# Layer 0 attention: pages issued by one engine, a ring of seven groups, the set-up moved

## The chip, the cores and the metric

The kernel runs on one core of a Trainium2 chip. A core has five engines with queues of their own: PE (matmul), DVE (VectorE), ACT (ScalarE), POOL (GpSimd) and SP, which only issues transfers and waits. They meet through semaphores. Sixteen DMA engines carry out what any of them issues. The metric is device time in microseconds of one execution, median of several.

## The reference, cut to what matters

One step of a two-layer decoder, for a prompt of 512 tokens and for 8 samples with 4 new tokens each. Layer 0 mixes two things: attention with forgetting (8 heads of 64) and a pooling mixer. The samples attend over 2048 past tokens, which lie in 16 pages of 128 tokens each, found through a page table.

```python
def gather_pages(pool, page_table):
    g = pool[page_table]
    return g.reshape((page_table.shape[0], page_table.shape[1] * pool.shape[1]) + pool.shape[2:])

def fox_attention(q, k, v, logf, pos0):
    cum = jnp.cumsum(logf.astype(jnp.float32), axis=1).transpose(0, 2, 1)
    ...
        logits = jnp.einsum('bqhd,bkhd->bhqk', qi, k, preferred_element_type=jnp.float32) * scale
        logits = logits + ci[..., :, None] - cum[:, :, None, :]
        mask = (k_pos[None, :] <= q_pos[:, None])[None, None]
        p = masked_softmax(logits, mask)
        return jnp.einsum('bhqk,bkhd->bqhd', p.astype(v.dtype), v)
```

For the samples k and v are the gathered pages of `cache_fox_k` and `cache_fox_v` with the new rows behind them: 8 samples x 16 pages x 2 caches = 256 pages, each 128 tokens x 512 numbers of 4 bytes, 256 KB.

## The kernel before

`fox_mixer` runs layer 0's mixer in stages, one behind the other, with all engines meeting between two stages (a stage's end clears its semaphores on POOL). The stages that matter here are the pooling mixer (`pooling`, 218 to 251 us of the trace) and the attention (`fox_prompt`, 252 to 512 us). Behind it comes the output projection.

In the attention stage two things share the engines. `prompt_attention` does the prompt: 8 heads x 4 tiles of 128 queries are 32 units, plus four "out" items, one item per step, and the phases of an item (scores, maximum, exponential, turn, values) lie some steps apart. Scores are four matmuls a unit: the query against the key's high part (KH) and low part (KL), a bias (SELB against B3, the sum of the forget gates in three parts) and a mask (ID against MASK). The keys' parts are made by ACT (L1739, L1740) and DVE (L1784, L1785), the queries by POOL (L1839, L1841).

Beside it `PastAttention` does the samples' past, in generators: each engine's generator moves one phase per step of the prompt, and runs on by itself when the prompt is done. A sample's 16 pages of keys are four groups of four pages, its values four more. The order of the 64 groups is fixed: keys of sample 0, then for each sample b the keys of b + 1 and the values of b. A turn is 11 phases: four with a key group, four with a value group, and three in which probabilities are turned and the output is finished. In the turn b = -1 only the keys of sample 0 are there, but it has 11 phases as well.

Groups land in a ring of four slots (`SLOTS`): two in RINGf and two in the free half of PT. `load` issues a group: for each page `value_load` reads the page's number into a register (L1336), then the page's transfer is issued (L1337). SP issues pages 0 and 2 of each group, POOL pages 1 and 3, each with a semaphore per slot. Group k waits until group k - 4 is used (`used`, raised by PE). SP issues the first four groups, then the stores of the new keys and values from TOK (`store_tokens`, which waits until they have landed), and then the rest. POOL first makes four queries and then issues, between its other work. PE waits for both halves in `landed`.

DVE starts the stage with its set-up (`setup` in `fox_prompt`): the values are copied to VE, B3 and SELB are made, then MASK and ID. Only then is `consts` raised, for which PE and ACT wait.

Of the kernel before, what the change touches and what calls it, by code (L numbers as in the profile page):

```python
# [999 lines left out]
class Mixers(Kernel):  # L1000
# [205 lines left out]
    def pooling(self, PT, meal):  # L1206
        nc, ps, i, o, H = self.nc, self.ps, self.i, self.o, self.H
        EX, NE = POOLW[-1] - 1, POOLW[-1] - 1 + TS
        with self.stage() as (sb, sem):
# [4 lines left out]
            ld, tr, ev, mm, st, dc, dd = (sem("pl_" + n) for n in ("ld", "tr", "ev", "mm", "st", "dc", "d"))  # L1214
            with nc.Block() as block:
# [14 lines left out]
                def _(pe):  # L1230
# [14 lines left out]
                    for g in range(4):  # L1245
# [4 lines left out]
                        last.then_inc(mm, 1)  # L1250

# [40 lines left out]

class PastAttention:

    R, PAGES, QUARTERS, SLOTS = FH * TS, PAST // PAGE, 4, 4
# [3 lines left out]
    def __init__(self, kernel, sb, sem, PT, TOK, NC, EP, first):  # L1299
# [4 lines left out]
        self.ring = sb("RINGf", [P, 2, self.QUARTERS, 512])  # L1304
# [9 lines left out]
        self.sp_full, self.pool_full = ([sem(f"fd_{n}_full{s}") for s in range(self.SLOTS)] for n in ("sp", "pool"))  # L1314
# [10 lines left out]
    def slot(self, k):  # L1325
        s = k % self.SLOTS
        return self.ring[:, s, :, :] if s < 2 else self.low[:, s - 2, :, :]

    def load(self, engine, parity, k):
        kind, b, n = self.groups[k]  # L1330
        if k >= self.SLOTS:
            engine.wait_ge(self.used, k - self.SLOTS + 1)
        pages = self.k.i["cache_fox_k"] if kind == "k" else self.k.i["cache_fox_v"][0].rearrange("n t h d -> n t (h d)")
        for a in range(parity, self.QUARTERS, 2):
# [3 lines left out]
                (self.pool_full if parity else self.sp_full)[k % self.SLOTS], 16)  # L1338

    def sp(self, sp, store):  # L1340
# [3 lines left out]
        for k in range(self.SLOTS):  # L1344
            self.load(sp, 0, k)
        store(sp)
        for k in range(self.SLOTS, len(self.groups)):
            self.load(sp, 0, k)
        self.k.start_out(sp, self.k.i["ab_w_out"][0], self.first)

    def pool(self, pool):
        for k in range(self.SLOTS):
            self.load(pool, 1, k)
        yield
        for b in range(-1, NB):
            for kind, of in (("k", b + 1), ("v", b)):
                for n in range(self.PER):
                    k = self.index.get((kind, of, n))
                    if k is not None and k + self.SLOTS < len(self.groups):
                        self.load(pool, 1, k + self.SLOTS)  # L1360
                    yield
            yield
            yield
            yield

    def pe(self, pe):
# [76 lines left out]
        for b in range(-1, NB):  # L1443
# [21 lines left out]
    def act(self, act):  # L1465
# [25 lines left out]
        for b in range(-1, NB):  # L1491
            for n in range(self.PER):
                yield
            for n in range(self.PER):
                if n == 0 and b + 1 < NB:
                    exponentials(b + 1)
                yield
# [9 lines left out]
    def dve(self, dve):  # L1507
# [50 lines left out]
        nc.vector.memset(RS[:, :], 0.0)  # L1558
        link(nc.vector.tensor_reduce(SAME[:, 0:R], self.k.ident.rearrange("p (a r) -> p r a", a=QUARTERS), AX.X, ALU.add))
# [10 lines left out]
        for b in range(-1, NB):  # L1570
# [4 lines left out]
            for n in range(self.PER):  # L1575
# [16 lines left out]
class Attention(Mixers):  # L1592

    def prompt_tiles(self, sb, sem, n_units, key_slots):
# [3 lines left out]
                 ID=sb("IDr", [P, P], F32R), MASK=sb("MASKr", [P, P], F32R), PC=sb("PC", [P, 3, P]))  # L1598
        T["KT"] = [(sb(f"KH{n}", [P, w], F32R), sb(f"KL{n}", [P, w], F32R)) for n, w in enumerate(key_slots)]
        names = ("consts", "queries", "q_high", "keys", "k_high", "scores", "maxima", "bank_read", "turned", "out_act", "out_dve", "valued", "combined",  # L1600
                 "added", "dc")
        return T, {n: sem("pa_" + n) for n in names}

    def prompt_attention(self, T, sems, groups, heads, keysets, outs, setup_dve, store, beside=None):
# [50 lines left out]
        with nc.Block() as block:  # L1655
# [5 lines left out]
            def _(pe):  # L1661
                if beside:
                    phases = beside.pe(pe)
                pe.wait_ge(sems["consts"], 1)
# [1258 lines left out]
```

## Time and profile before

| | |
|---|---|
| median of three runs | 2511.11 us (2507.73 to 2511.7) |
| span of the profiled execution | 2506.9 us |
| median less span | 4.2 us |
| PE busy | 2148.1 us (86%) |
| DVE, ACT, POOL busy | 1208.0, 579.4, 264.4 us |
| moved by DMA | 322.15 MB, mean 129 GB/s |
| attention stage of layer 0 | 251.97 to 511.88 us |
| pages moved in it | 256 x 256 KB |

The span runs from the first to the last instruction of the profiled execution; the runs' times have some start and end around it, so a change of the span is added to the median. Two views of the profile are used: groups (how much of a stretch an engine or the DMA engines were busy, who waited for whom, how long an instruction took) and the order of time. In the order of time "x4 3.70" stands for four instructions from the first one's start to the last one's end, and the brackets give the engine's idle time and what ended it. "SPq" is SP's queue of instructions.

### The profile page before, as it was taken

The numbers are of one execution on the slowest core, as the hardware profiler recorded it, in microseconds if no ns is written. First come the engines' busy times: TensorE is split into PE (matmuls) and PEld (weight loads), VectorE is DVE, ScalarE is ACT, GpSimd is POOL, SyncE is SP. The second block draws the span as 40 slices with busy tenths as digits, with TensorE's granted clock in tenths as the row PEclk, the third lists the DMA queues.
The fourth block names the chain that finished last, engine by engine and source line by source line (L and its number), as shares of the span: only waits on it lengthen the run. The fifth ranks groups of instructions, "written<-read, shape, count | busy, mean of one in ns | idle before, by whom it ended". The sixth has DMA issues, their size and how long they took to land. (4 is left out here: it accounts for less than half of the span.)

```text
span 2506.9 us, 49578 instructions
## 1 busy us (share of the span) xinstructions
PE 2148.1 (86%) x18597; PEld 1932.8 (77%) x18597; DVE 1208.0 (48%) x2280; ACT 579.4 (23%) x1074; POOL 264.4 (11%) x429
## 2 busy tenths in 40 slices
PE   4987697787999899698779996998987688999898
PEld 2863573475999899698469995988974487999898
DVE  4434531155444433443645657777743355444433
ACT  2220331012101000201135664444431211101000
POOL 0100423200000000000012222212223100000000
PEclk8986896688999999799779997998988898999999
DMA  9325778834323231223440003433448522223221
GB/s 354 112 63 220 242 246 322 308 118 136 92 84 92 84 101 52 62 68 113 203 151 2 1 2 112 123 115 103 121 160 324 216 64 74 86 85 91 87 92 59
DMA packets 237438, 322.15 MB, mean 129 GB/s; under 512 B 18235, under 2 KB 194440, under 8 KB 229807
## 3 DMA queue, kind: packets, MB, share of 16 engines
q1 hardware_dynamic: 215191, 239.29, 28.9%
q0 software_dynamic: 22048, 80.24, 9.3%
q8 instruction: 121, 1.98, 0.3%
q14 instruction: 78, 0.64, 0.1%
HBM read 311.56 MB, written 16.42 MB: 131 GB/s over the span
## 5 line engine op out<-in xcount | busy, mean ns | idle before, releaser
L441 PE MATMUL ps<-XHup,WHup 128*128 128x272 f32 x1408 | 293.2, 290 | 17.0 <-DVE XLup L415 13.5
L441 PE MATMUL ps<-XHup,WLup 128*128 128x272 f32 x1408 | 292.8, 290 | 0.0
L441 PE MATMUL ps<-XLup,WHup 128*128 128x272 f32 x1408 | 291.8, 289 | 0.0
L2279 PE MATMUL ps<-CHi,W1H 128*128 128x256 f32 x768 | 222.3, 289 | 37.5 <-DVE CLo L2382 37.5
L441 PEld LDWEIGHTS ps<-XHup,WHup 128*128 128x128 f32 x1408 | 222.7, 189 | 19.9 <-DVE XLup L415 14.3
L441 PEld LDWEIGHTS ps<-XLup,WHup 128*128 128x128 f32 x1408 | 222.7, 190 | 0.0
L441 PEld LDWEIGHTS ps<-XHup,WLup 128*128 128x128 f32 x1408 | 221.0, 190 | 0.0
L2280 PE MATMUL ps<-CLo,W1H 128*128 128x256 f32 x768 | 220.2, 287 | 0.0
L2281 PE MATMUL ps<-CHi,W1L 128*128 128x256 f32 x768 | 220.2, 287 | 0.0
L2279 PEld LDWEIGHTS ps<-CHi,W1H 128*128 128x128 f32 x768 | 150.5, 196 | 39.5 <-DVE CLo L2382 29.2
L434 DVE CAST WHup<-RAWup 128x1024 fp32r<-128x1024 f32 x88 | 61.1, 695 | 221.1 <-DMA RAWup<-in_w_up 164.5
L441 PE MATMUL ps<-GH,WHdn 128*128 128x272 f32 x704 | 148.5, 293 | 17.0 <-remote 15.1
L2280 PEld LDWEIGHTS ps<-CLo,W1H 128*128 128x128 f32 x768 | 150.4, 196 | 0.0
L2281 PEld LDWEIGHTS ps<-CHi,W1L 128*128 128x128 f32 x768 | 150.2, 196 | 0.0
L441 PE MATMUL ps<-GL,WHdn 128*128 128x272 f32 x704 | 147.4, 291 | 0.0
L441 PE MATMUL ps<-GH,WLdn 128*128 128x272 f32 x704 | 146.9, 290 | 0.0
L1797 DVE TENSOR_REDUCE NM<-ps 128x1 f32<-128x128 f32 (+1 forms) x224 | 89.6, 403 | 111.3 <-PE ps L1685 74.9
L441 PE MATMUL ps<-XHin,WHin 128*128 128x272 f32 x576 | 122.8, 295 | 19.3 <-issue 12.2
L1759 ACT ACTIVATE P<-ps,NM 128x128 f32<-128x128 f32 (+1 forms) x224 | 101.3, 458 | 139.3 <-DVE NM L1797 134.3
L441 PEld LDWEIGHTS ps<-GH,WHdn 128*128 128x128 f32 x704 | 112.5, 192 | 17.9 <-issue 17.9
L441 PE MATMUL ps<-XHin,WLin 128*128 128x272 f32 x576 | 121.3, 293 | 0.0
L441 PE MATMUL ps<-XLin,WHin 128*128 128x272 f32 x576 | 121.3, 293 | 0.0
(503 smaller groups left out, 4240.0 us busy)
## 6 DMA issues: line engine op xcount, KB each, us to landing
RAWup<-in_w_up SPq DMA_DIRECT2D x88, 512.0 KB, 3.8
Wearly<-in_w_mod SPq DMA_DIRECT2D x24, 1024.0 KB, 11.4
RAWdn<-in_w_down SPq DMA_DIRECT2D x14, 1408.0 KB, 6.5
RAWin<-in_nsa_w_in SPq DMA_DIRECT2D x20, 512.0 KB, 3.6
Wmod<-in_w_mod SPq DMA_DIRECT2D x8, 1024.0 KB, 16.9
RINGf<-in_cache_fox_k SPq DMA_DIRECT2D x32, 256.0 KB, 6.2
PT<-in_cache_fox_k SPq DMA_DIRECT2D x32, 256.0 KB, 6.1
RINGf<-in_cache_fox_k POOLq DMA_DIRECT2D x32, 256.0 KB, 5.7
```

Of the source, the lines that this page charges most:

```text
L434: link(self.nc.vector.tensor_copy(hi, values))
L441: mm = self.nc.tensor.matmul(self.ps[:, banks + n, 0:HALF], w, x[:, n * HALF:(n + 1) * HALF], start=start, stop=stop)
L1759: nc.scalar.activation(P3[:, n % 4, 0:w], ps[:, made[step] % S_BANKS, 0:w], ACT.Exp, bias=NM[:, n:n + 1]).then_inc(sems["bank_read"], 1)
L1797: nc.vector.tensor_reduce(NM[:, n:n + 1], ps[:, made[step] % S_BANKS, 0:width(*units[n])], AX.X, ALU.max, negate=True).then_inc(sems["maxi ...
L2279: nc.tensor.matmul(out, WH[:, sig, k, w], hi, start=(k == 0 and m == 0), stop=False, skip_group_check=True)
L2280: nc.tensor.matmul(out, WH[:, sig, k, w], lo, start=False, stop=False, skip_group_check=True)
L2281: last = nc.tensor.matmul(out, WL[:, sig, k, w], hi, start=False, stop=(k == KU - 1), skip_group_check=True)
```

## The change

- All 256 pages are issued by SP. `load` loses its `parity` and runs over all four pages; one semaphore per slot counts them. POOL's generator is gone.
- The ring has seven slots: three in RINGf, two in PT, and two more in TOK, whose rows are free once the stores have landed and the values are copied. `FIRST` is 5: SP issues five groups, then the stores, and groups 5 and 6 wait for `stored` and for the copy of the values.
- B3, SELB, ID and MASK are made by POOL in the pooling stage (`prompt_biases`); the tiles live in the outer stage.
- The values go to VE by ACT (`values`, behind the second key's copies); `consts` is not used where the samples' part runs beside the prompt. DVE clears QBA ahead of step 0.
- The turn b = -1 has 8 phases in place of 11: one in place of the four empty value phases.

```diff
-    def pooling(self, PT, meal):
+    def pooling(self, PT, meal, NC, bias):
...
+                @block.gpsimd
+                def _(pool):
+                    self.prompt_biases(pool, Chain(pool, made), PT, NC, *bias)
...
+    def prompt_biases(self, pool, link, PT, NC, B3, SELB, ID, MASK):
+        rest, middle, three = PT[0:FH, 8, 0:TP], PT[0:FH, 9, 0:TP].bitcast(F32R), PT[:, 10, 0:FH]
+        nc.gpsimd.tensor_copy(ID, self.ident)
+        nc.gpsimd.tensor_copy(MASK, self.dmask)
+        link(nc.gpsimd.tensor_tensor(three, self.ident[:, 0:FH], self.ident[:, 32:32 + FH], ALU.add))
+        link(nc.gpsimd.tensor_tensor(three, three, self.ident[:, 64:64 + FH], ALU.add))
+        nc.gpsimd.tensor_copy(SELB, three.unsqueeze(2).to_broadcast([P, FH, P]))
+        link(nc.gpsimd.tensor_scalar(B3, self.cos[:, 0:TP], 0.0, None, ALU.mult))
+        link(nc.gpsimd.tensor_copy(B3[0:FH, :], NC[:, 0:TP]))
+        link(nc.gpsimd.tensor_tensor(rest, NC[:, 0:TP], B3[0:FH, :].bitcast(F32), ALU.subtract))
+        link(nc.gpsimd.tensor_copy(middle, rest))
+        link(nc.gpsimd.tensor_copy(B3[32:32 + FH, :], middle.bitcast(F32)))
+        link(nc.gpsimd.tensor_tensor(B3[64:64 + FH, :], rest, middle.bitcast(F32), ALU.subtract))
...
-    R, PAGES, QUARTERS, SLOTS = FH * TS, PAST // PAGE, 4, 4
+    R, PAGES, QUARTERS, SLOTS, FIRST = FH * TS, PAST // PAGE, 4, 7, 5
...
+        self.rows_free = ((stored, 64), (valued, 1))
+        self.rows = TOK[:, 0:PT_TILES, :].rearrange("p t c -> p (t c)").rearrange("p (s a f) -> p s a f", s=2, a=self.QUARTERS)
...
-        return self.ring[:, s, :, :] if s < 2 else self.low[:, s - 2, :, :]
+        return self.ring[:, s, :, :] if s < 3 else self.low[:, s - 3, :, :] if s < 5 else self.rows[:, s - 5, :, :]
...
-    def load(self, engine, parity, k):
+    def load(self, engine, k):
         kind, b, n = self.groups[k]
         if k >= self.SLOTS:
             engine.wait_ge(self.used, k - self.SLOTS + 1)
+        elif k >= self.FIRST:
+            for signal, value in self.rows_free:
+                engine.wait_ge(signal, value)
...
-        for a in range(parity, self.QUARTERS, 2):
+        for a in range(self.QUARTERS):
             at = b * self.PAGES + self.PER * a + n
             page = engine.value_load(self.k.pages[0:1, at:at + 1], min_val=0, max_val=self.k.n_pages - 1)
             engine.dma_start(self.slot(k)[:, a, :], pages[ds(page, 1), :, :].rearrange("a p f -> p (a f)")).then_inc(
-                (self.pool_full if parity else self.sp_full)[k % self.SLOTS], 16)
+                self.full[k % self.SLOTS], 16)
...
-        for k in range(self.SLOTS):
-            self.load(sp, 0, k)
+        for k in range(self.FIRST):
+            self.load(sp, k)
         store(sp)
-        for k in range(self.SLOTS, len(self.groups)):
-            self.load(sp, 0, k)
+        for k in range(self.FIRST, len(self.groups)):
+            self.load(sp, k)
...
-    def pool(self, pool):
-        for k in range(self.SLOTS):
-            self.load(pool, 1, k)
...
         def landed(k):
-            pe.wait_ge(self.sp_full[k % self.SLOTS], 16 * QUARTERS // 2 * (k // self.SLOTS + 1))
-            pe.wait_ge(self.pool_full[k % self.SLOTS], 16 * QUARTERS // 2 * (k // self.SLOTS + 1))
+            pe.wait_ge(self.full[k % self.SLOTS], 16 * QUARTERS * (k // self.SLOTS + 1))
...
-            for n in range(PER):
+            for n in range(PER if b >= 0 else 1):
                 if b >= 0:
                     values(b, n)
...
+                        if values_act and k == keys_made[2]:
+                            values_act(act)
...
-            def setup(dve, link):
-                nc.vector.tensor_copy(VE[:, :, :, 0:HD], TOK[:, 0:PT_TILES, 512:1024].rearrange("p j (h d) -> p j h d", h=FH))
-                nc.vector.memset(VE[:, :, :, HD:HD + 1], 1.0)
...
+            def ones(dve, link):
+                nc.vector.memset(VE[:, :, :, HD:HD + 1], 1.0).then_inc(sems["values_dve"], 1)
+
+            def values(act):
+                nc.scalar.copy(VE[:, :, :, 0:HD], TOK[:, 0:PT_TILES, 512:1024].rearrange("p j (h d) -> p j h d", h=FH)).then_inc(sems["values_act"], 1)
```

On SP, at the first groups that wait for a used slot, the program before has two pages behind a wait (L1336 reads the number, L1337 issues):

```order
L1336 TENSOR_LOAD pages [waits fd_used_10]
L1336 ISA x2
L1337 ISA
L1337 DMA RINGf<-in_cache_fox_k 128x512
L1336 TENSOR_LOAD pages
L1336 ISA x2
L1337 ISA
L1337 DMA RINGf<-in_cache_fox_k 128x512
L1336 TENSOR_LOAD pages [waits fd_used_10]
```

and the changed program, where the two lines are L1361 and L1362, has four:

```order
L1361 TENSOR_LOAD pages [waits fd_used_10]
L1361 ISA x2
L1362 ISA
L1362 DMA RINGf<-in_cache_fox_k 128x512
L1361 TENSOR_LOAD pages
L1361 ISA x2
L1362 ISA
L1362 DMA RINGf<-in_cache_fox_k 128x512
...
L1361 TENSOR_LOAD pages [waits fd_used_10]
```

Two more pages stand there in the cut. The instructions of one page are the same five kinds in both.

On DVE, at the start of the attention stage, the program before has the set-up ahead of the first key's low part (L1784):

```order
L1869 COPY VE<-TOK 128x32x64
L1870 MEMSET VE 128x32
L1871 TENSOR_SCALAR B_10<-PT 128x512
...
L1879 CAST SELB<-three 128x1024
L85 ISA
L1775 CAST MASKr<-CN 128x128
L1776 CAST IDr<-CN 128x128
L85 ISA
L1784 TENSOR_TENSOR KL_10<-PT,KH_10 64x512
```

and the changed program has only clearing there:

```order
L1883 MEMSET VE 128x32
L1566 MEMSET QBA 128x1024
L1567 MEMSET RS 128x2
L1805 TENSOR_TENSOR KL_10<-PT,KH_10 64x512
```

The set-up's other instructions stand on POOL in the stage before, and the copy to VE on ACT behind its first exponential.

## Rows read from the trace of the kernel before

**Rows 1.** Busy us by stretch: PE PEld DVE ACT POOL (instructions), clock, DMA, GB/s
```profile
300.00:336.00 36.00, 31.66 (x337) 24.65 (x336) 13.17 (x35) 13.47 (x30) 12.28 (x20) 0.86 0.68 235
336.00:366.00 30.00, 28.53 (x342) 22.00 (x340) 12.98 (x38) 9.44 (x22) 8.58 (x16) 0.99 0.80 282
...
394.00:421.00 27.00, 20.30 (x234) 11.09 (x230) 3.47 (x14) 2.14 (x7) 8.58 (x16) 0.63 0.87 313
```

**Rows 2.** Waits of SP's queue, 250 to 515 us: total us, times, longest
```profile
SPq L1336 <- PE ps L1380: 69.8, 13, 15.6
SPq L1336 <- PE ps L1405: 18.1, 20, 1.8
```

**Rows 3.** Order of time, SP, start of stage: start, us, engine, line, operation
```profile
253.89 3.70 SPq L1337 DMA_DIRECT2D RINGf<-in_cache_fox_k  x4
...
258.35 3.63 SPq L1337 DMA_DIRECT2D PT<-in_cache_fox_k  x4
...
262.02 0.44 SPq L1195 DMA_DIRECT2D out_fox_k_p<-TOK  x1
...
274.79 3.71 SPq L1337 DMA_DIRECT2D RINGf<-in_cache_fox_k  x4
```

**Rows 4.** Lines L1336 and L1337, SP's queue: ns min/median/max
```profile
L1336 SPq TENSOR_LOAD <-pages x128: 262/269/498, 252.9 to 496.2; - x128
L1336 SPq FUSED_REGOPS  x128: 152/152/188, 253.4 to 496.5; - x128
...
L1337 SPq DMA_DIRECT2D RINGf<-in_cache_fox_k x32: 337/338/377, 253.9 to 462.0; - x32
```

**Rows 5.** Order of time, SP, later stretches
```profile
394.28 3.65 SPq L1337 DMA_DIRECT2D RINGf<-in_cache_fox_v  x4
...
398.70 3.64 SPq L1337 DMA_DIRECT2D PT<-in_cache_fox_v  x4
...
493.42 3.81 SPq L1337 DMA_DIRECT2D PT<-in_cache_fox_v  x4
...
1847.11 17.14 SPq L2155 DMA_DIRECT2D KS<-in_cache_nsa_ks  x16
```

**Rows 6.** Issue to landing, us: RINGf, 253 to 260; L1337, 394 to 403
```profile
DMA to landing us min/median/max: 2.7/2.9/3.1
...
DMA to landing us min/median/max: 2.6/5.3/6.4
```

**Rows 7.** Order of time, stage's start, and line L1999 of a later stage
```profile
252.02 1.67 DVE L1869 COPY VE<-TOK 128x2048 f32<-128x2048 f32 x1 [1.08 <-PEq L117]
...
252.69 2.11 POOL L1841 TENSOR_TENSOR QS<-PT,QS 64x512 fp32r<-64x512 f32 x1
...
263.23 0.25 DVE L1776 CAST IDr<-CN 128x128 fp32r<-128x128 f32 x1
...
266.36 0.44 PE L1680 MATMUL ps<-KH,QS 128*128 128x128 f32 x1 [16.25 <-DVE KL L1785]
...
L1999 ACT COPY VE<-TOK x2: 1037/1042/1047, 1244.2 to 1245.1; 128x1024 f32<-128x1024 f32 x2
```

**Rows 8.** Order of time, one turn's values and heads, and the stage's end
```profile
409.50 1.94 PE L1405 MATMUL ps<-PT,PTT 128*32 128x512 f32 x8 [0.61 <-DMA PT<-in_cache_fox_v]
...
411.37 1.91 PE L1415 MATMUL ps<-TOK,PTN 32*32 32x512 f32 x2
...
416.02 1.92 PE L1438 MATMUL ps<-SAME,Of 128*128 128x32 f32 x8
...
509.52 0.75 DVE L1546 TENSOR_SCALAR Of<-ps,W 128x512 f32<-128x512 f32 x1 [2.79 <-PE ps L1415]
...
511.53 0.35 DVE L1554 COPY H<-ps 64x16 f32<-64x16 f32 x2 [1.26 <-PE ps L1438]
```

**Rows 9.** Order of time, end of the pooling stage
```profile
237.74 0.17 DVE L1284 TENSOR_TENSOR Dl<-Dl,PT 128x16 f32<-128x16 f32 x1
...
244.87 5.24 PE L1249 MATMUL ps<-Dl,MAP 128*128 128x272 f32 x16
```

More of the change, by code:

```diff
@@ L1313, in __init__ @@
         self.const_in = sem("fd_const")
-        self.sp_full, self.pool_full = ([sem(f"fd_{n}_full{s}") for s in range(self.SLOTS)] for n in ("sp", "pool"))
+        self.full = [sem(f"fd_full{s}") for s in range(self.SLOTS)]
         self.used, self.queries, self.scores, self.maxima, self.probs = (sem("fd_" + n) for n in ("used", "queries", "scores", "maxima", "probs"))
@@ L1493, in act @@
                 yield
-            for n in range(self.PER):
+            for n in range(self.PER if b >= 0 else 1):
                 if n == 0 and b + 1 < NB:
@@ L1574, in dve @@
                 yield
-            for n in range(self.PER):
+            for n in range(self.PER if b >= 0 else 1):
                 if n == 1 and b >= 0:
@@ L1663, in _ @@
                     phases = beside.pe(pe)
-                pe.wait_ge(sems["consts"], 1)
+                else:
+                    pe.wait_ge(sems["consts"], 1)
                 for step in range(steps):
@@ L1684, in _ @@
                         if dense(g):
-                            last = nc.tensor.matmul(bank[:, i * P:w], ID[:, :], MASK[:, :], start=False, stop=True, skip_group_check=True)
+                            last = nc.tensor.matmul(bank[:, i * P:w], ID, MASK, start=False, stop=True, skip_group_check=True)
                         else:
-                            last = nc.tensor.matmul(bank[:, 0:span], ID[:, :], G["mask"][:, i, :], start=False, stop=True, skip_group_check=True)
+                            last = nc.tensor.matmul(bank[:, 0:span], ID, G["mask"][:, i, :], start=False, stop=True, skip_group_check=True)
                         last.then_inc(sems["scores"], 1)
@@ L1731, in _ @@
                     phases = beside.act(act)
-                act.wait_ge(sems["consts"], 1)
+                else:
+                    act.wait_ge(sems["consts"], 1)
                 for step in range(steps):
@@ L1774, in _ @@
                 setup_dve(dve, link)
-                nc.vector.tensor_copy(MASK[:, :], self.dmask)
-                link(nc.vector.tensor_copy(ID[:, :], self.ident))
-                dve.sem_inc(sems["consts"], 1)
+                if beside:
+                    next(phases)
+                else:
+                    nc.vector.tensor_copy(MASK, self.dmask)
+                    link(nc.vector.tensor_copy(ID, self.ident))
+                    dve.sem_inc(sems["consts"], 1)
                 for step in range(steps):
@@ L1826, in _ @@
                 placed = summed = 0
-                if beside:
-                    phases = beside.pool(pool)
                 for step in range(steps):
@@ L1853, in _, with fox_prompt @@
                         nc.gpsimd.tensor_tensor(dst, dst, T2[:, adds[g] % 2, :, :], ALU.add).then_inc(sems["added"], 1)
-                    if beside:
-                        next(phases, None)
-                for _ in phases if beside else ():
-                    pass
-    def fox_prompt(self, PT, TOK, NC, EP, first, store):
+    def fox_prompt(self, PT, TOK, NC, EP, bias, first, store, stored):
         nc, H = self.nc, self.H
         with self.stage() as (sb, sem):
-            T, sems = self.prompt_tiles(sb, sem, FH * PT_TILES, [TP] * 3)
-            past = PastAttention(self, sb, sem, PT, TOK, NC, EP, first)
+            B3, SELB, ID, MASK = bias
+            T, sems = self.prompt_tiles(sb, sem, FH * PT_TILES, [TP] * 3, (ID, MASK))
+            past = PastAttention(self, sb, sem, PT, TOK, NC, EP, first, stored, sems["values_act"])
@@ L1888, in fox_prompt @@
                                    value=lambda j, h=h: VE[:, j, h, :]))
-            self.prompt_attention(T, sems, groups, heads, keysets, [H[:, c, 0:TP] for c in range(4)], setup, lambda sp: past.sp(sp, store), past)
+            self.prompt_attention(T, sems, groups, heads, keysets, [H[:, c, 0:TP] for c in range(4)], ones, lambda sp: past.sp(sp, store), past, values)
     def gather(self, pool, table, col, where, dst, loaded):
@@ L1924, in fox_mixer @@
                 self.to_tokens(PT, 4, 8, TOK, 6)
-                self.pooling(PT, (self.early, 13))
-                self.fox_prompt(PT, TOK, NC, EP, first, lambda sp: self.store_tokens(sp, TOK, [("fox_k", 0, 512, 0), ("fox_v", 512, 512, 0)], stored))
+                self.pooling(PT, (self.early, 13), NC, bias)
+                self.fox_prompt(PT, TOK, NC, EP, bias, first,
+                                lambda sp: self.store_tokens(sp, TOK, [("fox_k", 0, 512, 0), ("fox_v", 512, 512, 0)], stored), stored)
 class Trunk(Attention):
```

44 lines of the change are left out of this document (15 added, 29 removed).

## The prediction

> **What bounds the kernel now.** I read three views in this order: the busy table of stretches, the waits of SP's queue, and the order of time. The change touches the layer 0 attention stage (252 to 512 us) and the end of the pooling stage before it. Nothing else moves, so the question is what sets the end of that stage. From 394 to 421 us, one sample's turn of eight page groups, PE is busy 20.3 of 27 us at a granted clock of 0.63, while the DMA engines are busy 0.87 of the time and move 313 GB/s [rows 1]: pages, not arithmetic. With prompt work beside it a turn takes 30 us (336 to 366, clock 0.99) and the first one 36 us [rows 1]. SP is not short of time now: it waits 69.8 + 18.1 us for a ring slot, that is for PE to finish with a group [rows 2]. POOL issues the other half of the pages. So today the rate comes from PE and the DMA engines together, through four slots, and SP has slack. The change takes away the half that gives SP its slack, so the first number that I need is the time that SP takes to issue one page.
>
> **SP's price of a page.** At the stage's start SP issues eight pages with no wait and no POOL beside it: the first starts at 253.89, the last ends at 258.35 + 3.63, so it starts at 261.64 (an issue is 0.338 us long [rows 4]); (261.64 - 253.89) / 7 = 1.107 us from one page to the next [rows 3]. Other stretches agree: four pages from 394.28 to 398.70 give 1.105, and sixteen pages of another cache (half the bytes) took 17.14, so (17.14 - 0.34) / 15 = 1.120 [rows 5]. The instructions themselves are shorter: 0.269 to read the page number, 0.152 for the address, 0.338 to issue [rows 4], 0.76 in sum with two tiny ones left out; the rest of the interval stands between them as time of the sequencer. The size of the transfer hardly enters. I take 1.107.
>
> **Part 1, all 256 pages on SP.** Before, SP and POOL issue 128 each. A group is four pages, 4.43 us of SP alone, and a turn of eight groups 35.4 us, against 27 to 30 us that a turn now takes. The issue becomes the bound. Its chain: first page at 253.89 as before (nothing of the change is ahead of it on SP). Five groups go ahead of the stores, 20 pages, the last at 253.89 + 19 x 1.107 = 274.92. The first store is issued 0.38 us behind the last page's start (before: 262.02 after 261.64), so at 275.30. From the first store to the first page behind the stores it was 274.79 - 262.02 = 12.77 us [rows 3]: four issues, then a wait until all four have landed and nothing else is issued. I keep it: next page at 288.07. The new wait on ScalarE's copy of the values ends earlier than that (ScalarE reaches it behind the prompt's first unit, and 30 us are left). The 236 pages left need 235 x 1.107 = 260.1: last page at 548.2. Before, the last was issued at 493.42 + 3.81 - 0.34 = 496.9 [rows 5]. That is **+51.3 us**.
> Does anything hold SP back beyond this? Group k needs group k - 7 to be used. That one was issued 31 us earlier and landed some 24 us earlier than the slot is needed, while the stretch of a turn in which PE uses no group, from the new rows' values at 411.37 to the heads' end at 416.02 + 1.92, is 6.6 us [rows 8]. So no stall, and I add none. If the issue is the bound, PE has 35.4 us for turns that took 27 to 30; only the first, at 36 us [rows 1], could cost 1 us more.
> First the trace, then a rule, on whether the issue matters at all. Alone, a page lands 2.9 us after its issue, beside POOL's pages 5.3 us [rows 6]; transfers overlap, and at 313 GB/s a page of 262 KB takes the engines 0.84 us, less than SP's 1.107. The Trainium skill, DMA: Bandwidth & Descriptors, section Issuing engines are not separate DMA queues, says that issuing from several engines saves only the sequencer's time for the issue, "which is usually small relative to the DMA itself". By that rule giving up POOL's queue costs nothing; by the rows the issue is longer than the engines' share of the transfer, and the 51 us stand. What the rule would give is rival A, and it is a reason to give that rival a chance at all. The same page's table of latencies states a floor of about 600 ns for tensor_load; with 0.338 that would be an estimated 0.94 us a page and a stage only some 4 us longer. The rows show 0.269 for that instruction but 1.107 for the whole, so I don't use it.
>
> **Part 2, the tail.** Before, 15.0 us pass from the last issue (496.9) to the last copy's end (511.53 + 0.35 = 511.88) [rows 8], since PE was behind. After, PE waits for the last page: 2.9 us of landing [rows 6], then at the durations of the stretch with a granted clock of 0.63, 1.94 us of values, 1.91 of the new rows' values, 0.75 and 0.15 for the output's scaling, 1.92 for the heads [rows 8] and 0.35 for the copy, with small gaps 7.2 us. 2.9 + 7.2 = 10.1, so **-4.9 us**. The first block of the output weights is issued right behind the last page and lands before the stage ends.
>
> **Part 3, the biases.** VectorE's setup goes: from 252.02 to 263.23 + 0.25 it worked, ScalarE waited for it, and PE began at 266.36 [rows 7]. Eleven instructions move to POOL, the 1.67 us copy to ScalarE (two copies of half the size took 1.04 each elsewhere: 2.1 us). What is late next for the prompt: the key's two copies and two differences, 1.25 + 1.4 us, and POOL's first query at 252.69 + 2.11 = 254.8. So PE starts near 255, 11.4 us earlier. Three empty steps go too; at 30 us for 11 steps [rows 1] that is 3 x 2.7 = 8.2 us. Neither shows in the end: PE's step 0 then needs group 0, whose fourth page is issued at 257.2 and lands at 260.1; groups 1 to 3 follow at 4.43 us each, and then group 5 only at 288.07 + 3.3 + 2.9 = 294.3. The work stands on the pages. I book **0**, and 19.6 us if the issue were not the bound (rival A).
> In the pooling stage POOL is idle. Eleven instructions at no more than 2.11 us, POOL's dearest row, [rows 7] are under 24 us from 217.8, so done by 242; the stage runs to 251. VectorE's steps there may slow down beside POOL. VectorE ended at 237.74 + 0.17, PE takes its result at 244.87 [rows 9]: 6.8 us of cover. Between 0 and, if all of VectorE's work there from 224 to 238 were 1.5 times as long, 0.2 us over the cover; I take 0.
> That POOL leaves the pages also frees its descriptor work; nobody waits for that now except the pages themselves.
>
> **Sum.** +51.3 - 4.9 + 0 = +46.4 us: span 2506.9 + 46.4 = 2553.3. The median of the runs is 4.2 us above the span, so **2557.5 us**.
>
> **Rivals.**
> A, the issue is not the bound (ends faster). If without POOL's queue SP's interval fell, the start's 11.4 + 8.2 us would come through and the time would be 2511.1 - 19.6 = 2491.5. It decides at one number: SP's last issue may be at 501.8 (10.1 before 511.9); less 253.89, 0.38 and 12.77 this leaves 234.8 us for 254 intervals, 0.924 us each. Under 0.924 the stage is not longer; below some 0.85 the consumers set the end. For it: the three named instructions sum to 0.76 us. Against it: the eight pages at 253.89 were issued while POOL issued nothing, at 1.107. Chance 0.05.
> B, an interval between the two, no difference that can be told: 5 us either way are 0.02 us of the interval, 0.904 to 0.944, and 2506 to 2516. No stretch of the rows has it. 0.03.
> C, slots bind again. SP's longest wait for PE is 15.6 us; three slots more cover 13.3; if seven turns still lost the 2.3 us left, the time is 2557.5 + 16 = 2573. For it: the coupled turns at 36 us. Against it: the account of the slots above. 0.07.
> The forecast has 0.85.
>
> **How the numbers follow.** Unknown sizes within the forecast: the interval 1.100 to 1.120 (-1.8, +3.3); the stores without POOL's pages beside them, 2.1 MB at 313 GB/s and 1.5 us of issues, 8.5 us in place of 12.77 (-4.3), above the same; the tail at the upper clock (-2.5) and landing at 5.3 (+2.4); the first turn (+1). Together 2549 to 2564. The range takes in part of C and some more below: 2547 to 2568. Runs of this kernel tell 0.2%, 5 us, from no change. Slower by more: forecast and C, 0.92; within: B, 0.03; faster: A, 0.05.
>
> **What would show it.** SP's issues 4.4 us a group from 288 to 548 with hardly a wait on `used`; PE waiting for pages all through; DMA near 237 GB/s where it was 313; PE's first unit near 255; its first values behind 290; the stage's end near 558. Wrong if the page interval comes out under 1.0, or if SP waits for slots by more than 5 us in sum.

## The result, and the profile after

| | before | changed |
|---|---|---|
| median of four runs each | 2509.42 us (2502.79 to 2511.7) | 2568.24 us (2562.25 to 2574.37) |
| ratio to before | | 1.0236 [1.0211, 1.0261] |
| span of the profiled execution (its run) | 2506.9 us | 2560.6 us (2562.25) |
| attention stage, its start to the next stage's start | 252.0 to 516.4, 264.4 us | 254.5 to 565.9, 311.4 us |

Slower by 2.4%, as forecast; the size was forecast as 46.4 us and is 58.8. The median lies 10.7 us above the forecast and 0.24 us above the top of the range.

The order of time on SP at the stage's start; it answers to [rows 3]:

```profile
256.42 12.50 SPq L1362 DMA_DIRECT2D RINGf<-in_cache_fox_k  x12
269.68 8.43 SPq L1362 DMA_DIRECT2D PT<-in_cache_fox_k  x8
278.15 0.44 SPq L1195 DMA_DIRECT2D out_fox_k_p<-TOK  x1
...
287.40 4.86 SPq L1362 DMA_DIRECT2D TOK<-in_cache_fox_k  x5
```

and at its end, the last group and the first block of the output weights:

```profile
547.39 3.63 SPq L1362 DMA_DIRECT2D RINGf<-in_cache_fox_v  x4
551.07 0.43 SPq L1907 DMA_DIRECT2D RAWout<-in_ab_w_out  x1
```

The first 20 pages start between 256.42 and 269.68 + 8.43 - 0.34 = 277.77, 1.124 us apart. The last page starts at 547.39 + 3.63 - 0.34 = 550.68, so that the 235 intervals behind the stores are (550.68 - 287.40) / 235 = 1.120 us. (The view at the stage's start ends at 292 us, so it has five of the eight TOK pages.) Hardly anything of it is waiting. The waits of SP's queue in the stage (total us, times, longest), which answer to [rows 2]:

```profile
SPq L1357 <- DMA out_fox_v_s<-TOK: 4.7, 1, 4.7
SPq L117 <- PEq L117: 4.6, 3, 3.5
SPq L1361 <- PE ps L1414: 1.7, 7, 0.3
SPq L1361 <- PE ps L1389: 0.7, 3, 0.3
```

For a used slot SP now waits 2.4 us, where it waited 87.9. The one longer wait is that for the stores. PE waits in its place, for pages, 71.0 us in sum, in ring, TOK and PT alike:

```profile
PE ps L1414 <- DMA RINGf<-in_cache_fox_v: 26.4, 11, 3.0
PE ps L1414 <- DMA TOK<-in_cache_fox_v: 16.1, 9, 3.2
PE ps L1389 <- DMA PT<-in_cache_fox_k: 9.7, 5, 3.2
PE ps L1389 <- DMA TOK<-in_cache_fox_k: 8.5, 5, 3.0
PE ps L1414 <- DMA PT<-in_cache_fox_v: 8.4, 6, 2.6
...
PE ps L1389 <- DMA RINGf<-in_cache_fox_k: 1.9, 2, 1.1
```

Busy time by stretch (the columns of [rows 1]): one turn beside the prompt and two of the samples alone.

```profile
336.00:371.00 35.00, 29.25 (x338) 22.37 (x337) 12.11 (x36) 10.99 (x25) 0.00 (x0) 0.95 0.78 237
406.00:442.00 36.00, 22.72 (x238) 12.63 (x242) 3.47 (x14) 2.73 (x8) 0.00 (x0) 0.62 0.79 238
442.00:477.00 35.00, 21.65 (x218) 11.13 (x210) 3.46 (x14) 2.14 (x7) 0.00 (x0) 0.56 0.78 234
```

The rate is the same, 234 to 238 GB/s, with the prompt and without it, at a granted clock of 0.95 and of 0.56. What the consumers do in these stretches doesn't move it. A page of 262 KB at 237 GB/s is 1.106 us.

The stage's start shows that the moved set-up did what it says; beside [rows 7], on PE:

```profile
258.07 0.48 PE L1692 MATMUL ps<-KH,QS 128*128 128x128 f32 x1 [5.53 <-DVE KL L1806]
...
264.86 0.65 PE L1389 MATMUL ps<-RINGf,QBA 128*32 128x128 f32 x8 [5.67 <-DVEq L85]
```

PE's first unit comes 3.6 us behind the stage's start, where it came 14.3 us behind it (266.36 - 252.02). Its first page group, at 264.86, waited for VectorE (DVEq L85) and not for pages; the third (272.65) and the fourth (276.57) wait for their pages, and from there on the work goes at SP's rate.

### The profile page after: what moved, and what is told of

It reads as the page before. It is cut to its first block and busy times, and to the rows that moved or that the text cites. A ratio compares the mean times of both kernels' runs of the same rounds, so it can differ in the third digit from the quotient of the medians.

```text
span 2560.6 us, 49521 instructions
## 1 busy us (share of the span) xinstructions
PE 2166.4 (85%) x18597; PEld 1941.3 (76%) x18597; DVE 1202.1 (47%) x2268; ACT 581.9 (23%) x1075; POOL 206.5 (8%) x312
```

## The experiments

The theory: SP's time to issue a page, about 1.1 us, is the bound of the stage, and the slots, the moved biases and the short turn have nothing to do with the loss. Rivals: the ring's new slots or POOL's new work cost the time; or the bytes themselves are at their limit; or PE and the slots set the end whatever SP does. All times are medians, with the ratio to the kernel before as it ran on the same chip.

**The same kernels again.** No edit.

> The changed kernel once more, beside the others and with more rounds. In the profiles compared so far the attention stage accounts for 47 us of the difference (start to next stage's start 264.4 us before, 311.4 us after), while the medians are 59 us apart; 2.5 us came ahead of the stage and some 4 us behind it, in code that the change doesn't touch. If these are scatter between executions, the ratio settles near 1.019 to 1.022 (2557 to 2565). If the change costs something in the other stages too (placement of tiles, say), it stays at 1.0235 (2568) or above and the same stages are longer again.

> The kernel before, unchanged, for a second profile of it. The first one showed 120.3 us for the stage from 51 to 171 us where five profiles of other kernels with the same code there showed 123.6. If that is scatter, this one shows about 123.6 too and 2511 us in all; the attention stage stays at 264 to 266 us.

The changed kernel: 2572.07 us, ratio 1.0242 [1.0226, 1.0258]; its profiled stage took 315.5 us. The kernel before: 2511.49 us, 1.0005 [0.9991, 1.0019]; stage 261.6 us, shorter than the 264 expected, and the attention starts 4.3 us later than in the first profile. So one profile of a stage is good to some 4 us. The ratio went neither to 1.019 nor to 1.022, so the loss outside the stage is no accident of one pair of profiles; it is taken up below. The interval behind the stores was 1.136 us in the second profile of the changed kernel: eight pages take 8.02 us most of the time, as in the first profile, and in both some take 8.4 in place of it, in the second one also 8.8, 9.4 and 10.1.

**SP alone, and nothing else of the change.** The kernel before, ring of four and set-up on VectorE as they were:

```diff
-        for a in range(parity, self.QUARTERS, 2):
+        for a in range(self.QUARTERS):
...
-    def pool(self, pool):
...
-            pe.wait_ge(self.sp_full[k % self.SLOTS], 16 * QUARTERS // 2 * (k // self.SLOTS + 1))
-            pe.wait_ge(self.pool_full[k % self.SLOTS], 16 * QUARTERS // 2 * (k // self.SLOTS + 1))
+            pe.wait_ge(self.sp_full[k % self.SLOTS], 16 * QUARTERS * (k // self.SLOTS + 1))
```

> The kernel before with that one part alone: SP issues all four pages of a group, POOL none; ring of four, set-up on VectorE. Theory: 64 groups at 4.45 us and the stores' wait give SP's last page near 547 to 551 as in the changed kernel, since SP starts at the same place and is the bound in both: 2555 to 2568 us. With four slots SP could wait a little for slots on top, up to 2575. Rival 1 (the other parts make the loss): 2515 or less.

2570.37 us, ratio 1.0225 [1.0207, 1.0243]; stage 316.3 us. The issue alone makes the whole loss, and the other parts give nothing on top of it: four slots are enough for a queue this slow (SP waited 4.7 us for used slots, 2.3 us more than with seven).

**Everything but SP alone.** The changed kernel with pages 1 and 3 of each group back on POOL, ring of seven:

```diff
-        for k in range(self.FIRST):
-            self.load(sp, k)
+        for k in range(self.FIRST):
+            self.load(sp, k, (0, 2))
...
+    def pool(self, pool):
+        for k in range(self.SLOTS):
+            self.load(pool, k, (1, 3))
+        yield
...
+            pe.wait_ge(self.pool_full[k % self.SLOTS], 16 * 2 * (k // self.SLOTS + 1))
```

> The changed kernel with one part undone: POOL issues pages 1 and 3 of each group again, SP pages 0 and 2. Ring of seven, biases in the pooling stage, values by ScalarE and the short first turn stay. Theory (SP's 1.12 us for a page sets the stage): the whole loss goes and the start's gain, about 20 us, comes through: 2490 us, 0.99 of before. Rival 1 (the loss is from the other parts: slots in TOK that wait for the stores, biases on POOL beside VectorE): it stays above before, 2540 or more. Rival 2 (no start gain in any case since PE and the DMA engines set the turns): 2505 to 2511.

2481.13 us, ratio 0.9878 [0.9863, 0.9893], 9 us less than expected; stage 230.9 us, 80 us shorter than with SP alone. The other parts of the change are worth 30 us, once the issue is not the bound. In the stretch of 390 to 420 us, and on POOL's queue there:

```profile
390.00:420.00 30.00, 20.88 (x250) 10.43 (x242) 3.95 (x17) 3.24 (x11) 12.99 (x25) 0.75 1.03 386
```

```profile
390.69 0.54 POOL L1362 DMA_DIRECT2D PT<-in_cache_fox_k  x1 [0.61 <-issue]
391.84 0.54 POOL L1362 DMA_DIRECT2D PT<-in_cache_fox_k  x1 [0.61 <-issue]
```

386 GB/s, against 234 to 238. A page costs POOL 1.15 us (391.84 - 390.69), as much as it costs SP: two queues, half of the time.

At the stage's start the two queues do worse than SP alone. POOL makes its four queries first and issues its first page 9.6 us behind the stage's start, and PE, ready early, waits for that half of the first group. First this run, then the kernel before:

```profile
264.99 0.65 POOL L1362 DMA_DIRECT2D RINGf<-in_cache_fox_k  x1 [0.23 <-issue]
...
272.48 0.66 PE L1405 MATMUL ps<-RINGf,QBA 128*32 128x128 f32 x8 [12.40 <-DMA RINGf<-in_cache_fox_k]
```

```profile
271.59 0.66 PE L1380 MATMUL ps<-RINGf,QBA 128*32 128x128 f32 x8 [4.14 <-DVEq L85]
```

Counted from the stage's start the first page group is used after 19.6 us in the kernel before, 17.1 here and 10.4 in the changed kernel. So as long as POOL issues half of the pages behind its queries, the moved set-up brings the samples' part forward by 2.5 us and not by 11.4.

**The same with a ring of four.** This parts the ring from the moved set-up:

```diff
-    R, PAGES, QUARTERS, SLOTS, FIRST = FH * TS, PAST // PAGE, 4, 7, 5
+    R, PAGES, QUARTERS, SLOTS, FIRST = FH * TS, PAST // PAGE, 4, 4, 4
```

> half2 with a ring of four slots (FIRST 4): so the kernel before with biases in the pooling stage, values by ScalarE and the short first turn, POOL issuing its half. It measures what the moved set-up and the three phases give: by the prediction's part 3, 11.4 + 8.2 = 19.6 us, 2492 us. What half2 (2481) has on top of that would be the ring of seven. If instead the ring gives nothing, four is at 2481 as well.

2501.63 us, ratio 0.9971 [0.9958, 0.9985]; its profiled stage took 248.3 us (that run was its fastest, 2489.59 us, and is no measure of the median). Expected for the set-up and the short turn were 19.6 us, and 2492 us in all. By the medians they give some 7 us, and the ring of seven another 23 (0.9971 - 0.9878 of 2510); by the profiles 13 to 16 and 17. Here too the first page group waits for its pages (13.9 us, to 18.6 us behind the stage's start), so that most of the 11.4 us expected at the start doesn't come through. What the ring is worth shows in the waits of SP's queue, first with four slots, then with seven:

```profile
SPq L1361 <- PE ps L1405: 54.3, 16, 9.6
SPq L1361 <- PE ps L1430: 18.6, 17, 2.2
```

```profile
SPq L1361 <- PE ps L1405: 30.5, 9, 8.1
...
SPq L1361 <- PE ps L1430: 6.8, 8, 2.2
```

**Three pages on SP, one on POOL.** The page split alone is changed against the run with half of the pages on POOL:

```diff
-            self.load(sp, k, (0, 2))
+            self.load(sp, k, (0, 1, 2))
...
-                        self.load(pool, k + self.SLOTS, (1, 3))
+                        self.load(pool, k + self.SLOTS, (3,))
```

> Like half2, but SP issues three pages of each group and POOL one. Theory (SP's interval of 1.12 to 1.14 us sets the stage only where it comes to more than PE and the DMA engines need): SP needs 3.4 us a group, 27 us a turn, the stores' wait on top; the last page near 483, the stage 235 to 240 us, 5 to 8 us longer than with the half (230.9), time 2484 to 2492 and under before. A rival in which any page moved from POOL to SP costs in proportion (half of the 90 us between half2 and again2) gives 2526.

2488.22 us, ratio 0.9916 [0.9899, 0.9933]; stage 241.5 us. SP waited 0.3 us for a slot, and three pages took it 3.31 us over and over, 3.40 in the mean behind the stores: still SP's queue, at 0.85 us per page of the whole stream. The stage's length in us follows SP's count of pages (4, 3, 2 a group: 311 to 315, 241.5, 230.9) down to three, and not below: with two something else is the bound. Beside the prompt PE is busy 28.4 of 30 us there (300 to 330 us), and behind it the pages come at 380 to 386 GB/s; no run parts these two.

**What in the issue costs the time.** First the changed kernel without any read of a page number, SP alone:

```diff
-            page = engine.value_load(self.k.pages[0:1, at:at + 1], min_val=0, max_val=self.k.n_pages - 1)
-            engine.dma_start(self.slot(k)[:, a, :], pages[ds(page, 1), :, :].rearrange("a p f -> p (a f)")).then_inc(
+            engine.dma_start(self.slot(k)[:, a, :], pages[at:at + 1, :, :].rearrange("a p f -> p (a f)")).then_inc(
```

> The changed kernel with the page numbers written into the program in place of read from the page table: SP issues all 256 pages, but no register is read. It reads other pages than the table names, so its samples' attention is over other tokens; the bytes and the number of transfers are the same. Theory (the reading of the number and the address arithmetic make up two thirds of the 1.12 us): the interval falls to 0.34 to 0.5 us, SP waits for slots again, the stage is set by PE and the DMA engines and the time is 2480 to 2495. Rival (one hardware queue moves pages no faster than 237 GB/s, whatever the instructions): SP stays the bound through its queue and the time stays at 2555 to 2570.

2476.08 us, ratio 0.9853 [0.9836, 0.987], 4 us below the expected range; stage 220.5 us. SP waits for slots again (32.3 + 6.9 us). SP's order of time at the start, for the same twelve pages that took 12.50 us, and the stretch from 390 to 420 us:

```profile
256.05 6.44 SPq L1361 DMA_DIRECT2D RINGf<-in_cache_fox_k  x12
```

```profile
390.00:420.00 30.00, 23.86 (x303) 15.54 (x306) 5.49 (x22) 3.21 (x10) 0.00 (x0) 0.69 1.05 386
```

One queue moves 386 GB/s as well. So it is not that one queue can't carry the bytes, nor that POOL's queue was needed for them: what costs is the sequencer's work ahead of each transfer. 12.50 - 6.44 over 11 intervals is 0.55 us a page for reading a number and forming an address, half of the interval; two thirds were expected. That this stage is shorter than the 230.9 us with two queues goes with its start: the first page group is used 10.4 us behind the stage's start, 6.7 us earlier.

Then a kernel that keeps the page table: the number is read for the key page and kept in its register for the value page.

```diff
-            page = engine.value_load(self.k.pages[0:1, at:at + 1], min_val=0, max_val=self.k.n_pages - 1)
+            if kind == "k":
+                self.numbers[at] = engine.value_load(self.k.pages[0:1, at:at + 1], min_val=0, max_val=self.k.n_pages - 1)
+            page = self.numbers[at]
```

> The changed kernel, but a page's number is read once: keys and values of a sample lie in the same pages, so the value pages use the register (and address) that the key pages left. SP still issues all 256 pages, POOL none. Theory: a key page costs 1.12 to 1.14 us, a value page as with numbers in the program 0.48 to 0.56, a turn of 32 pages 26 to 27 us, no more than PE and the DMA engines need; stage 220 to 240 us, time 2473 to 2492, level with half2 or better. Rival (something else in SP alone makes the loss, the queue or the missing half of POOL): 2555 or more.

2501.57 us, ratio 0.9977 [0.9966, 0.9989]; stage 247.3 us. Key pages and value pages in one turn, SP alone:

```profile
401.40 8.48 SPq L1364 DMA_DIRECT2D PT<-in_cache_fox_k  x8
409.98 3.98 SPq L1364 DMA_DIRECT2D TOK<-in_cache_fox_v  x8
```

Eight pages with the read take 8.48 us, eight without it 3.98. With 0.82 us a page on average behind the stores SP alone is no longer slower than the kernel before. The prediction's threshold, 0.924 us, is thereby bracketed (1.12: 2.4% slower; 0.82: 0.2% faster), though not hit. The expectation was missed: the time lies 10 us above its range and 20 us above the run with half of the pages on POOL, and the stage above its 240. The turn of 32 pages was foreseen well, about 26.5 us (32 x 0.82), but it was taken for no more than PE and the DMA engines need. They need less. SP hardly waits for slots, and PE waits for pages:

```profile
SPq L1364 <- PE ps L1391: 1.5, 5, 0.5
SPq L1364 <- PE ps L1416: 0.5, 1, 0.5
```

```profile
PE ps L1416 <- DMA TOK<-in_cache_fox_v: 10.9, 5, 2.8
PE ps L1416 <- DMA RINGf<-in_cache_fox_v: 10.7, 10, 2.4
```

So SP's queue is still the bound at 0.82 us a page, where the prediction let the consumers set the end below 0.85.

Both together, half of the pages on POOL and the numbers read once:

> POOL issues pages 1 and 3 of each group again (as in the run with half of the pages on POOL) and each page number is read once, for the key page and the value page of a slot (as in the run that reads once). If the queues' instructions still limit the stage when two queues issue, the stage falls below that run's 230.9 us, to about the 220.5 us that the run without any read showed: about 2471 us, 2466 to 2476. If in that run the transfers themselves were already the bound (their share of the 16 engines was 0.96 to 1.03 there, at 333 to 386 GB/s), nothing is left for shorter issues: 2481 us, 2477 to 2485.

2478.97 us, ratio 0.9887 [0.9869, 0.9906]; stage 227.7 us, within the 2477 to 2485 of the expectation's second case: no difference to the 0.9878 with two reads. Two queues with reads are fast enough for what stands behind them. SP waits for PE there (38.6 + 14.0 us), and the stretch from 390 to 420 us moves 386 GB/s with a DMA share of 1.04.

**Where the rest comes from.** The stage grew by 50.4 us (mean of two profiles each: 313.4 less 263.0), the median by 59 to 60. Of the start of the last common stage less the attention stage, six profiles in which POOL issues pages have 2228.2 to 2238.5 us, mean 2234.7, and six in which SP alone does 2237.7 to 2245.0, mean 2242.8. Somewhat more than half of these 8 us is one stage, the decode stage of layer 1 (1867 to 2002 us before), which the change doesn't touch: 135.0 to 136.4 us, mean 135.8, in the first six profiles, and 135.8 to 142.8, mean 140.4, in the other six. The first run puts POOL's reads back and no transfer:

```diff
+    def read(self, pool, k):
+        kind, b, n = self.groups[k]
+        for a in (1, 3):
+            at = b * self.PAGES + self.PER * a + n
+            pool.value_load(self.k.pages[0:1, at:at + 1], min_val=0, max_val=self.k.n_pages - 1)
```

> The changed kernel, in which POOL also reads the page numbers of slots 1 and 3 at the places where it issued pages before, and issues nothing. SP still issues all pages. It asks where the 8.5 us outside the attention stage come from (2234.1 us in the five profiles in which POOL issues pages, 2242.6 us in the five in which SP alone does). If they hang on POOL's program (what POOL executes, and where it lies), the sum outside the stage goes back to about 2234 us: 2563 us. If they hang on the pages' queue, it stays near 2243 us: 2572 us, as the changed kernel measured. Inside the stage both expect SP's interval of 1.12 to 1.14 us a page; were POOL's reads in SP's way, it would rise above that.

2571.45 us, ratio 1.0252 [1.0234, 1.027]; stage 312.6, the rest 2244.1, the decode stage 141.8 us. POOL's reads of the page numbers have no part in it. The order of time on PE in that decode stage shows stops that nothing releases ("issue"), here in this run:

```profile
1959.29 3.09 PE L2592 MATMUL ps<-VS,SST 128*32 128x64 f32 x105 [4.37 <-issue]
1990.12 3.63 PE L2592 MATMUL ps<-VS,SST 128*32 128x64 f32 x125 [4.36 <-issue]
2023.17 0.44 PE L2592 MATMUL ps<-VS,SST 128*32 128x64 f32 x8 [4.69 <-issue]
2029.11 0.65 PE L2592 MATMUL ps<-VS,SST 128*32 128x64 f32 x16 [1.99 <-issue]
```

and in the run with half of the pages on POOL:

```profile
1909.03 1.07 PE L2587 MATMUL ps<-VS,SST 128*32 128x64 f32 x28 [4.69 <-issue]
1938.73 1.51 PE L2587 MATMUL ps<-VS,SST 128*32 128x64 f32 x48 [3.92 <-issue]
1965.81 1.20 PE L2587 MATMUL ps<-VS,SST 128*32 128x64 f32 x67 [0.81 <-issue]
```

The runs of matmuls behind the stops are as long in every kernel with one wait per group (105, 124 or 125, 8, 16, 35 or 36), and again in every kernel with two (28, 47 or 48, 67). The runs without any read and with POOL's reads, which change the programs of SP and POOL, leave them where they were. With SP alone PE's program has 64 waits fewer. The second run gives them back, with nothing to wait for:

```diff
         def landed(k):
             pe.wait_ge(self.full[k % self.SLOTS], 16 * QUARTERS * (k // self.SLOTS + 1))
+            pe.wait_ge(self.full[k % self.SLOTS], 16 * QUARTERS * (k // self.SLOTS + 1))
```

> The changed kernel, in which PE's wait for a page group stands twice (the second one is already fulfilled), so that PE's program has as many waits in the attention stage as where POOL issues half of the pages. Nothing else. In the decode stage of layer 1 PE stands without a releaser at fixed places of its matmuls: in all five profiles with one wait per group behind 105, 125, 8, 16 and 36 matmuls of a row (two stops of 4 + 2 us a turn), in the profiles with two waits behind 28, 47 or 48 and 67 (one stop a turn). If the place of PE's later instructions sets this, the 64 more waits move the stops to 28, 48 and 67, that stage goes from 142 back to about 136 us, and the time from 2571.5 to about 2564 us, at a page interval that stays 1.12 to 1.14 us. If the stops come from the transfers' queues, they stay at 105, 125, 8, 16, 36, and so does the time: 2571 us, 2569 to 2573.

2565.68 us, ratio 1.0239 [1.0222, 1.0256]; stage 313.0, the rest 2232.0, the decode stage 134.5 us. The stops moved as the theory of the place wants it:

```profile
1986.26 0.64 PE L2566 MATMUL ps<-VS,SST 128*32 128x64 f32 x28 [3.88 <-issue]
...
2016.50 1.50 PE L2566 MATMUL ps<-VS,SST 128*32 128x64 f32 x48 [4.50 <-issue]
2043.07 1.20 PE L2566 MATMUL ps<-VS,SST 128*32 128x64 f32 x67 [0.81 <-issue]
```

So the place of these stops hangs on how many instructions PE has ahead of them. That this costs the missing 8 us is not shown. The first profile of the changed kernel has its stops at the places of one wait per group, and its decode stage took 135.8 us all the same. And against before on their chips, the medians are 60.0 us above it with the waits doubled, 60.5 and 61.9 without, which their intervals don't part, and the profiled run of the doubled waits was its lowest (2558.1). That PE waits for its instructions at these places is only argued. What the part of the loss outside the attention stage consists of in a typical run stays open.

## Why the prediction was right or wrong

**The bound, right.** The rows that carried it were SP's unattended start and the sequencer's gaps [rows 3, 4]. What the last part of the prediction asked for came: SP at 4.4 to 4.5 us a group with hardly a wait, PE waiting for pages, 234 to 238 GB/s, PE's first unit early, the stage's end at 561.3 where 558 was asked for. The run with SP alone and nothing else lost the same 2.2 to 2.4%, and the runs that took instructions away from the issue got it back.

**The sum, too low.** What failed is its size, in two terms. The larger is "Nothing else moves": everything outside the attention stage was booked at nothing, and it grew by 8 us. It takes 2242.8 us in the mean of six profiles with SP alone against 2234.7 in six with two queues, and the medians grew by 58.8 us where the stage grew by 50.4 (mean of two profiles each). The cause of these 8 us is open; the runs show only that they come with SP alone also where the rest of the change is missing, that POOL's reads are not their cause, and that somewhat more than half of them lies in the decode stage. The smaller term is the stage itself, 46.4 us forecast and 50.4 measured, and in it the interval. Together they are 8.4 + 4.0 = 12.4 us of the difference; the median is only 10.7 us too high because that of the kernel before came out 1.7 us lower with one run more. The range held nothing for a growth elsewhere.

The profiled execution, whose span is 7.3 us above the forecast 2553.3, step by step:

| step | predicted | measured | adds |
|---|---|---|---|
| first page | 253.89 | 256.42 | +2.5 |
| 19 intervals and to the first store | 21.4 | 21.7 | +0.3 |
| first store to next page | 12.77 | 9.25 | -3.5 |
| 235 intervals | 260.1, 1.107 each | 263.3, 1.120 each | +3.1 |
| last page to the last copy's end | 10.1 | 10.6 | +0.5 |
| from there to the end of the span | 1995.0 | 1999.3 | +4.3 |

The interval is the term of the stage that was mis-sized: 1.107 came from eight pages at the start, and 235 of them average 1.120, in the second profile 1.136. I had the 1.120 as the end of my range and nothing above it. A mean over many intervals holds the slow ones, eight pages don't. The gap at the stores went the other way, which by luck cancels the interval's miss in this profile, and near the end of its range (8.5): SP's wait for them was 4.7 us, with no page of POOL beside the stores. The 2.5 us at the start are scatter of the stages ahead: over all profiles the attention stage starts between 250.0 and 256.3 us, in the second profile of before at 256.3. The last row doesn't come from the decode stage, which in this profile took as long as before (135.8 and 135.5 us). It comes between the attention's end and that stage: 1350.0 us in the first profile of before, 1354.4 here, but 1353.2 in the second profile of before, so that most of the 4.3 us is a short first profile.

**From the span to the median, wrong in its form.** I added 4.2 us, the median of before less the span of its profile. But a run lies 1.65 us above its own span (2562.25 and 2560.6, and so in every run that lists both); the other 2.6 us only said that the profiled run of before was a low one. For the changed kernel the profiled run was the lowest of four, and the median lies 6.0 us above it. The account of the whole: 2557.5 + 7.3 - 2.6 + 6.0 = 2568.2.

**The tail, right.** The values, the new rows' values and the heads took what they had taken:

```profile
554.26 1.93 PE L1414 MATMUL ps<-RINGf,PTT 128*32 128x512 f32 x8 [3.03 <-DMA RINGf<-in_cache_fox_v]
...
560.92 0.36 DVE L1563 COPY H<-ps 64x16 f32<-64x16 f32 x2 [2.10 <-PE ps L1447]
```

**The biases at nothing, right.** POOL's eleven instructions ended long before its stage did. The dearest was not at 2.11 us but at 2.54, beside a step of 2.35 us on VectorE; the same form of copy took 0.60 and 0.70 us in the two other places:

```profile
222.50 2.16 POOL L1306 TENSOR_SCALAR B<-CN 128x512 fp32r<-128x512 f32 x1
...
227.01 2.54 POOL L1309 CAST PT<-PT 8x512 fp32r<-8x512 f32 x1 [0.16 <-POOL PT L1308]
...
230.57 1.35 POOL L1311 TENSOR_TENSOR B<-PT 8x512 fp32r<-8x512 f32 x1 [0.17 <-POOL B L1310]
```

VectorE beside it was slowed, one step of 0.68 us to 1.52 (first before, then changed), and the same steps took 0.68 again once POOL was done. The cover held: the stage before the attention took 34.3 us, where it took 34.1.

```profile
227.61 0.68 DVE L1281 SCALAR_TENSOR_TENSOR Dl<-UP,PT 128x496 f32<-128x496 f32 x1
```

```profile
230.92 1.52 DVE L1285 SCALAR_TENSOR_TENSOR Dl<-UP,PT 128x496 f32<-128x496 f32 x1
```

**Rival C, refuted:** 2.4 us of waits for slots; that the time came near its 2573 is chance. **Rival A, right in kind and wrong in size.** It decides at the interval, and the run that reads once crossed the threshold. But I priced what it frees at 19.6 us, all of it from the start and the short turn, and the runs gave about 30, of which the ring has the larger part. Of the 11.4 us at the start little was there to be had while POOL's half of the first group came behind its queries. The rows had it: 87.9 us of waits for slots [rows 2] I read as SP's slack, where they also said that four slots kept both queues back. The Trainium skill's rule (DMA: Bandwidth & Descriptors, Issuing engines are not separate DMA queues), that several issuing engines save only the sequencer's time, which is usually small relative to the DMA, holds in its first half: without the reads SP alone does as well as two queues with them (2476 and 2481 us). The second half doesn't hold for these pages: 1.12 us of sequencer against 262 KB at 386 GB/s, 0.68 us. The floor of about 600 ns that the Trainium skill gives for tensor_load (the same page, Latency and other measured facts) is near the 0.55 us that a page saves without number and address, though the instruction itself has 0.27 in the rows.

## What to carry to other kernels

Before transfers are moved to one queue, take the time from one issue to the next from the longest stretch in which that queue waits for nothing, over the whole chain with its register reads, and set it against the time in which its consumers want the bytes; a busy share of the DMA engines near 0.8 doesn't say that they are the bound. If the queue is too slow, take instructions out of the issue first (read a page's number once for everything that it names: (3.98 - 0.34) / 7 = 0.52 us against 1.1 us a page here, where nothing holds SP back), or share the pages among queues. Here the parts of the change pay only in that order: with half of the pages left on POOL the same ring and set-up give 1.2% over the kernel before, with SP alone nothing. And before some microseconds in a stage that nobody touched are given to the change, more than one profile of each kernel is wanted, and a look at the places where an engine stands without a releaser: both differed here without a price that the runs could part.

## What was unexpected

- The DMA share hides slack: 0.78 at 237 GB/s, 0.87 at 313 [rows 1], 1.03 and 1.05 at 386 GB/s. The last two are over 1, and the first would promise only 304 GB/s.
- A transfer's issue instruction is itself not constant: without reads, where SP runs ahead of the transfers, it took 0.33 us at least, 0.43 in the median and up to 1.59, here for two of the tiles (ns min/median/max):

```profile
L1361 SPq DMA_DIRECT2D RINGf<-in_cache_fox_k x60: 327/432/1330, 256.1 to 401.0; - x60
...
L1361 SPq DMA_DIRECT2D PT<-in_cache_fox_v x36: 327/433/1589, 290.1 to 445.2; - x36
```

- PE's stops without a releaser, up to 4.8 us each, stand at places set by the number of instructions ahead of them, and 64 more waits in one stage move them in another 1400 us later.
- PE's granted clock was 0.56 to 0.62 in the changed kernel's turns of the samples alone and 0.63 in one before [rows 1], though the pages came at 234 to 238 GB/s in the one and at 313 in the other. What it cost can't be told here, since PE waited for pages in both.
